# A third weight buffer for tile 1 and a later copy of an attention pair, in a two-layer diffusion trunk

## The reference

```python
mx = (silu(c) @ ada_w[i] + ada_b[i])                       # nine modulation vectors
x = x + 0.5 * mx[2] * swiglu(modulate(rms_norm(x, g0), mx[0], mx[1]), w_gu0, w_down0)
s = concat([q @ k_loc * scale + bias, q @ k_ctx * scale]); p = softmax(s)
o = p[:n_loc] @ v_loc + p[n_loc:] @ v_ctx
```

## Time and profile before

| what | us |
|---|---|
| median of 3 runs (lowest to highest) | 2806.9 (2805.73 to 2807.57) |
| the profiled execution, own time | 2806.72 |
| its span | 2804.9 |
| PE busy in the span | 2674.8 |
| DVE, POOL, ACT busy | 1447.6, 928.8, 748.4 |

### The profile page before, as it was taken

How to read it: one execution, slowest core, us unless ns; L and a number is a source line. 1 busy time by engine, 2 the same in 40 slices (tenths; PEclk the granted TensorE clock), 3 DMA queues, 4 the chain that set the end, 5 groups by cost and what they waited for, 6 DMA issues and landing times. The chain is left out here.

```text
span 2804.9 us, 40607 instructions
## 1 busy us (share of the span) xinstructions
PE 2674.8 (95%) x15151; PEld 2492.1 (89%) x15151; DVE 1447.6 (52%) x2479; ACT 748.4 (27%) x1014; POOL 928.8 (33%) x438
## 2 busy tenths in 40 slices
PE   6999999999989899999999999999999986899998
PEld 5999999999958899999999999999998875778887
DVE  6666466565363666556656323422237885432233
ACT  4111122222163322111122221111225664332222
POOL 1323232322322232322232555355421112344442
PEclk8999999999999999999999999999998998999999
DMA  6444333422301233434442456445413322233232
GB/s 213 126 126 124 96 120 120 127 84 73 113 24 31 75 120 120 133 95 125 120 126 77 126 162 182 133 150 157 130 61 113 127 98 73 69 91 104 86 102 82
DMA packets 439330, 309.32 MB, mean 110 GB/s; under 512 B 9853, under 2 KB 414166, under 8 KB 439254
## 3 DMA queue, kind: packets, MB, share of 16 engines
q1 hardware_dynamic: 439254, 308.32, 36.1%
HBM read 278.92 MB, written 30.46 MB: 110 GB/s over the span
## 5 line engine op out<-in xcount | busy, mean ns | idle before, releaser
L802 POOL TENSOR_TENSOR w_lo<-raw,w_hi 128x1024 fp32r<-128x1024 f32 (+2 forms) x272 | 742.1, 2729 | 1457.5 <-ACT w_hi L938 1457.5
L938 ACT ACTIVATE w_hi<-raw 128x1024 fp32r<-128x1024 f32 (+2 forms) x272 | 310.0, 1140 | 1145.6 <-PE pair_b L1820 664.2
L1288 DVE TENSOR_TENSOR work_g<-work_s,pair_b 128x768 f32<-128x768 f32 (+1 forms) x88 | 78.1, 888 | 660.4 <-PE pair_b L1820 499.1
L1248 DVE SCALAR_TENSOR_TENSOR ada_sums<-ada_raw,cvec,ada_sums 128x256 f32<-128x256 f32 x896 | 395.6, 516 | 0.0
L1820 PE MATMUL pair_a<-h_hi,w_hi 128*128 128x384 f32 x1312 | 340.0, 340 | 9.9 <-POOL w_lo L802 9.8
L1820 PE MATMUL pair_a<-h_lo,w_hi 128*128 128x384 f32 x1312 | 335.6, 336 | 0.0
L1820 PE MATMUL pair_a<-h_hi,w_lo 128*128 128x384 f32 x1312 | 334.9, 336 | 0.0
L1820 PE MATMUL pair_b<-h_hi,w_hi 128*128 128x384 f32 x1168 | 296.6, 334 | 0.0
L1820 PE MATMUL pair_b<-h_hi,w_lo 128*128 128x384 f32 x1168 | 296.4, 334 | 0.0
L1820 PE MATMUL pair_b<-h_lo,w_hi 128*128 128x384 f32 x1168 | 296.3, 334 | 0.0
L1820 PEld LDWEIGHTS pair_a<-h_hi,w_hi 128*128 128x128 f32 x1312 | 235.7, 189 | 19.8 <-issue 9.7
(11 more groups left out here) (305 smaller groups left out, 4358.6 us busy)
## 6 DMA issues: line engine op xcount, KB each, us to landing
raw<-in_ffn_w_gu_dram SPq DMA_DIRECT2D x176, 512.0 KB, 3.9
ada_raw<-in_ada_w_dram SPq DMA_DIRECT2D x64, 1024.0 KB, 5.1
raw<-in_ffn_w_down_dram SPq DMA_DIRECT2D x64, 704.0 KB, 4.6
unit_raw<-in_rg_w_in_dram SPq DMA_DIRECT2D x40, 256.0 KB, 3.7
ada_first<-in_ada_w_dram SPq DMA_DIRECT2D x4, 2048.0 KB, 13.5
raw<-in_ab_w_in_dram SPq DMA_DIRECT2D x16, 512.0 KB, 3.9
u_split_dram<-unit_hi SPq DMA_DIRECT2D x20, 256.0 KB, 2.0
u_split_dram<-unit_lo SPq DMA_DIRECT2D x20, 256.0 KB, 2.3
```

What stands on the lines that cost most here:

```text
L802: nc.gpsimd.tensor_tensor(wl[:, par, 0:kt * P], raw[:, par, 0:kt * P], wh[:, par, 0:kt * P].bitcast(F32), ALU.subtract).then_inc(split_rea ...
L938: nc.scalar.activation(wh[:, par, 0:kt * P], raw[:, par, 0:kt * P], ACT.Copy).then_inc(hi_done, 1)
L1248: step = nc.vector.scalar_tensor_tensor(out=sums[v], in0=tiles(k), scalar=c_k, in1=sums[v], op0=ALU.mult, op1=ALU.add)
L1288: nc.vector.tensor_tensor(gbuf[:, 0, 0:W], sbuf[:, 0, 0:W], up, ALU.mult)\
```

## The change

Two buffers `third_w_hi` and `third_w_lo` are placed over the last 8192 bytes per partition of the FFN's g region (where the first modulation columns and, later, g_lo lie). They hold the gate panel of tile 1 of `gu00`. ACT fills the high one inside the opening, between its rows of contraction tiles 0 to 3 and those of 4 to 7; POOL fills the low one; PE's tile 1 reads them in place of buffer 0. ACT then does silu of tile 0 first and makes only panel 3 high after it. In attention, `take_heads` moves from DVE's step j = 1 to j = 2, and `heads_high` from ACT's step j = 2 to j = 3. All other waits stay as they are.

```diff
--- before.py
+++ after.py
@@ -238,6 +238,9 @@
         cvec_pad = later("cvec_padded", [P, KD, QUAD])
         quads = later("quad_sums", [P, 3, 2])
         ada0 = alias(g_at, g_end)("ada_first", [P, KD, 2 * ADA0 * P])
+        third = alias(g_end - 2 * size([P, KD * P]), g_end)
+        third_hi = third("third_w_hi", [P, KD * P], F32R)
+        third_lo = third("third_w_lo", [P, KD * P], F32R)
 
 
         att = alias(g_at, g_end)
@@ -840,7 +843,12 @@
             def ffn(f):
                 low(split_no(first[f"gu{f}0"]), 0, KD)
                 low(split_no(first[f"gu{f}0"]) + 1, 1, KD)
-                pairs(first[f"gu{f}0"], 1, KC, KD)
+                if f == 0:
+                    pool.wait_ge(hi_done, 3)
+                    nc.gpsimd.tensor_tensor(third_lo[:, :], raw[:, 0, 0:KD * P], third_hi[:, :].bitcast(F32), ALU.subtract)\
+                        .then_inc(split_ready, 1)
+                    low(3, 1, KD)
+                pairs(first[f"gu{f}0"], 1 + int(f == 0), KC, KD)
                 pairs(first[f"dn{f}0"], 0, KD // 2, KC)
                 pairs(first[f"gu{f}1"], 0, KC, KD)
                 pairs(first[f"dn{f}1"], 0, KD // 2, KC)
@@ -953,11 +961,9 @@
                 p0, F0 = first[f"gu{f}{h}"], GU_BEFORE[f, h]
                 if p0 == 0:
 
-                    for r in range(2):
-                        act.wait_ge(panel_used, r + 1)
-                        high(2 + r)
-                        if r == 0:
-                            silu(F0, p0)
+                    silu(F0, p0)
+                    act.wait_ge(panel_used, 2)
+                    high(3)
                 with act.Fori(int(p0 == 0), KC - 1) as i:
                     silu(i + F0, i * 2 + p0)
                     for r in range(2):
@@ -1096,6 +1102,8 @@
                         copy_ada0(3, pC, 512)
                 if half == 0:
                     copy_ada0(2, pB, 512)
+            act.wait_ge(raw_landed[0], 32)
+            nc.scalar.activation(third_hi[:, :], raw[:, 0, 0:KD * P], ACT.Copy).then_inc(hi_done, 1)
             act.wait_ge(coef_done, 2)
             for half in range(2):
                 for k in range(4, KD):
@@ -1131,7 +1139,7 @@
                 if s >= 1:
                     for a in range(2):
                         copy_turned(s - 1, a)
-                if j == 2 and t >= 1:
+                if j == 3 and t >= 1:
                     heads_high(t - 1)
             for a in range(2):
                 copy_turned(len(STEPS) - 1, a)
@@ -1704,7 +1712,7 @@
                 if s >= 1:
                     for a in range(2):
                         normalise(s - 1, a)
-                if j == 1 and t >= 1:
+                if j == 2 and t >= 1:
                     take_heads(t - 1)
             for a in range(2):
                 normalise(len(STEPS) - 1, a)
@@ -1814,7 +1822,10 @@
             def k_tile(ps, par, k, kt, hi, lo, W):
                 if W == SEQ:
                     return passes(ps[:, 0:SEQ], par, k, hi[:, k, 0:SEQ], lo[:, k, 0:SEQ], k == 0, k == kt - 1)
-                w1, w2 = wh[:, par, k * P:(k + 1) * P], wl[:, par, k * P:(k + 1) * P]
+                if par is None:
+                    w1, w2 = third_hi[:, k * P:(k + 1) * P], third_lo[:, k * P:(k + 1) * P]
+                else:
+                    w1, w2 = wh[:, par, k * P:(k + 1) * P], wl[:, par, k * P:(k + 1) * P]
                 for w, of, begins, ends in ((w1, hi, k == 0, False), (w1, lo, False, False), (w2, hi, False, k == kt - 1)):
                     for a in (0, HALF):
                         last = nc.tensor.matmul(tokens(ps, a, a + HALF), w, of[:, k, a:a + HALF], start=begins, stop=ends)
@@ -1921,7 +1932,7 @@
                     pe.wait_ge(silu_done, i + (F0 + 1))
                     if h == 1:
                         pe.wait_ge(resid_done, UPD[f"dn{f}0"] + KD - 1)
-                    panel(pA, 0, KD, hh, hl, W)
+                    panel(pA, None if isinstance(i, int) and p0 == 0 else 0, KD, hh, hl, W)
                     if mid is not None:
                         begin_group(GROUP_OF[name])
                         use_ada(mid, name)
```

## The result

The changed kernel takes **2793.9 us** (median of 5 runs, 2791.92 to 2796.63) against 2806.9 (median of 5 runs beside them, 2805.73 to 2807.57): a ratio of 0.995, 95% interval 0.9938 to 0.9961. It is faster by 13.0, the forecast was 2793.9. The profiled execution, the fastest of the five, took 2791.92 with a span of 2790.1, 14.8 under that of before.

What follows compares the result with a forecast made beforehand. PE bounds the kernel, busy 2674.8 of 2804.9 us. Third buffer 5.2 plus attention copy 7.8 make 13.0 off the median: 2793.9 us; forecast's own range 2791 to 2797, full range 2789.5 to 2799.5.

Steps and rivals of the forecast that it cites:

- the 5 and the 4: Prediction wrong if the attention stretch shrinks by less than 5 us or tile 2's start moves by less than 4.
- Part one: Split of the recurrent weights: not in the diff, already stored split before, so it costs and brings nothing.
- Part two: Third buffer in the opening: 6.8 us gained less 1.55 lost, about 5.2.
- The gain of 6.8: Tile 1 of the first FFN no longer waits for low weights: 4.9 us of idle and 1.9 of clock.
- The cost of 1.55: GpSimd's new low part in the opening holds VectorE 2.14 us; less slack of 0.6, PE loses 1.55.
- case C: Silu of tile 0: switching the function table costs 1.4 us more than its 1.28, giving 2795.3; chance 0.03.
- Part three: Attention, the pair's copy one step later: 1.94 us of idle plus 0.7 of clock, 2.6 a pair, 7.8.
- late biases: Attention: GpSimd's low part and six bias pieces slip; of 1.68 us of clock a pair, only 0.7 is counted.
- Case A: Opening: nothing blocks VectorE, so the third buffer gives 6.8 us and the kernel 2792.3; chance 0.15.
- B: Attention: the wait only moves, values wait for the copy, 1.2 us a pair left; 2798.1; chance 0.12.
- D: One part brings nothing: third buffer alone 2801.7 us, attention alone 2799.1; chance 0.07.
- E: Attention steps 10 and 11: low part and biases hold VectorE's normalising 5.5 us a pair; slower, 2808.8; chance 0.03.

Runs made afterwards that it cites:

- e9: The changed kernel with the third buffer's low part in four pieces and the heads' high parts back at step j = 2: 2793.37 us, ratio 0.9951.
- e10: e9 plus a third buffer for tile 1 of the second FFN: 2787.94 us, ratio 0.993.
- a0: The changed kernel once more, timed beside e9 and e10: 2793.13 us, ratio 0.9952.
- e2: The kernel before with only the attention order changed, without the third buffer: 2800.14 us, ratio 0.9975.
- e7: The changed kernel with the heads' high parts back at j = 2, the copy staying late: 2789.11 us, ratio 0.9939.
- e3: The kernel before with 11 useless transposes filling PE's wait at each pair's second step: 2804.37 us, ratio 0.9995.
- e1: The changed kernel with the attention order of before, so the third buffer only: 2801.07 us, ratio 0.998.
- e4: The changed kernel with the pair's copy and high parts one more step later: 2814.75 us, ratio 1.0035.
- e8: The changed kernel with 14 useless transposes on PE at attention's start and behind the opening panels of the second and fourth FFN: 2792.8 us, ratio 0.9945.
- e6: The changed kernel with GpSimd's low part of the third buffer in four pieces: 2790.38 us, ratio 0.9944.
- e5: The changed kernel with zeros written in place of the third buffer's low part: 2789.19 us, ratio 0.9938.

## Why the prediction was right

The total came out to a tenth, closer than its terms deserve: two errors of half a microsecond cancel (5.67 for 5.2, 7.38 for 7.8), and the changed kernel's second measurement gave 2793.1. That it came out to a tenth is luck; that it came out to a microsecond is not, since both parts gained where and how the prediction has it. The attention shrank by 7.4 and tile 2 moved by 7.4, above the 5 and the 4 that it had named as its limits. By its own steps:

- **Part one, nothing.** The parts alone sum to 12.0 of 13.0, and its row is unchanged.
- **Part two, 5.2: measured 5.67.** The gain of 6.8 held: idle of 5.03 and 1.9 of clock are gone whole, 6.9 (no idle was left where I had put 0.15). The cost of 1.55 was 1.29: opening start to opening end 17.83 before, 19.12 after. The hold explains it: VectorE's later rows moved back by 1.9 against the opening's start, less the slack of 0.6 that is 1.3, and without the long hold the opening takes 17.9 (e9, e10). My 1.55 has the hold at 2.14, the time that the steps themselves last (2.13), and forgets that they take 0.24 of it anyway.
- **A wrong step with no price.** I had silu of tile 0 wait for panel 0 and then 1.28 for the function table, ending just as PE comes free. The load in fact ran at 63.25, ahead of the wait, and silu ended at 65.72, 1.1 before PE was free. I had it end 0.1 behind PE and put the idle at 0.15; there was none. Of case C's 1.4 more for a switch, after the Trainium skill, "ScalarE: Activation LUTs", section "What ACT_TABLE_LOAD costs", no row shows anything: between the load's end and silu lies 0.38 here, which the row puts down to PE, and 0.02 before.
- **GpSimd's panel 3** ended at 72.43, 3.4 before PE wanted it. Hidden, as stated.
- **Part three, 2.6 a pair, 7.8: measured 7.38.** PE's step at the pair's end lost 1.93 (1.94 forecast) and the clock went to 1.00. From pair to pair the gain is 3.08, 2.53 and 2.73, 8.34 in all, plus 0.27 behind the last; 1.23 was lost at the start of the attention, where the idle is the same as before but half clock lasted longer (in such executions the first pair's step is 0.4 shorter: 17.06 here, 17.44 in a0). e2 and a0, with less of that, show 8.3 and 8.2. What I took back for late biases, 1.0 a pair, is 0.3 by e7, and an unbroken clock is worth 0.9 a pair by e3, not the 1.68 that I had counted. The two terms were both too large; their difference, put at 0.7, measured 0.85 (8.34 / 3 - 1.93), and 0.7 in e2 and a0 (2.67 and 2.65 a pair). So the size of this term was right by two errors that cancel.
- **Case A** (nothing blocks VectorE) fell with the row of 2.13; e9 and e10 show that it would have given 1.2 to 1.3. The measured hold agrees with the Trainium skill, "SBUF — State Buffer", section "SBUF: two separate sides", that a VectorE step with two SBUF inputs and a GpSimd operation that reads SBUF exclude each other for a whole instruction: the steps last until the piece that is running ends when the work comes in pieces (0.61), and until the end of all of it when it doesn't (2.13). **B**: its place showed no idle at all. **C**: see the table load above. **D**: e1 and e2 each gain. **E**: not here, but e4 shows its chain, one step on.

## What to carry to other kernels

Price a move by the whole chain that hangs on the moved step: the copy one step later won 1.9 a pair in idle and cost 0.3 in later biases, one step further it lost 20 us, and VectorE stood 11.4 us for biases, three steps down the chain. A third buffer for the first tile after a serial stage pays for its idle and for the half clock behind that; its low part on GpSimd cost 1.2 to 1.3 less in pieces, by the traces, though no time proves it. And take a window's lost clock as the upper end of what it is worth: 1.68 was read here, 0.9 came back, and at the start of the attention some 3 us at half clock cost nothing.

## What the runs showed of the hardware that I had not expected

- **The same idle time is not followed by the same half clock.** At the start of the attention PE idles 2.27 and 1.01 in both kernels; the clock was low until about 793 before (3.3 us) and until 788.4 after (6.6 us). An idle of 1.88 in the attention was followed by half clock twice in e1 and not the third time. One of 1.88 in the second FFN was followed by it (e8), one of 2.63 in the fourth by none. Windows, the kernel after, then before:

```profile
781.00:789.00 8.00, 6.99 (x35) 0.57 0.01 2
```

```profile
789.00:793.00 4.00, 3.67 (x13) 0.58 0.00 0
```

Why it differs stays open; it moves single executions by 1 to 2 us, as much as the finer edits here.

- **Where a table load stands hangs on how the step is written.** In a loop (e9, second FFN) it ran at 948.97, behind a wait of 1.74 for PE. Written ahead of the loop (e10) it ran at 945.58, before the wait. So silu began 1.29 after PE had released it in the one and at once in the other. The loads at this line also fall from 31 to 22: the nine steps left in that loop have none of their own. PE waited for no silu there in either kernel, so this is no part of e10's gain.
- **Pieces let VectorE in, at a small price.** The subtraction in four pieces held the two small VectorE steps for 0.4 in place of 1.9 (e6), and took GpSimd 2.82 in place of 2.38. In e9 a later VectorE step, an h_lo at 54.56, was held as well (1.02 in place of 0.62); PE waited for neither. Whether a zero fill holds VectorE isn't shown: e5's ended as the steps began.
